# A mixture-of-experts block on one core: big buffers at new addresses, splits of 2048 columns, and another order of work in expert block 0

## What is computed

```python
logits = hf @ w_router + b_router
top_vals, top_idx = lax.top_k(logits, 4); gates = softmax(top_vals)
# tokens sorted by expert into blocks of 128 rows, one expert a block
gu = xb @ w_gate_up[e] + b_gate_up[e]          # 1024 -> 2048
gate = minimum(gu[:, :1024], 7.0); up = clip(gu[:, 1024:], -7.0, 7.0)
act = (up + 1) * (gate * sigmoid(1.702 * gate))
y = act @ w_down[e] + b_down[e]                # 1024 -> 1024
out = segment_sum(y * gate_weight, token)      # and x is added
```

## Time and profile before

| | |
|---|---|
| profiled execution | 1751.46 us, span of the core 1749.6 us |
| runs | 1752.5 to 1759.7, median 1757.2 us |
| granted TensorE clock, mean | 0.987 |
| TensorE busy | 1700.0 us |
| VectorE busy | 1426.3 us |
| ScalarE busy | 1076.2 us |
| GpSimd busy | 248.2 us |
| HBM traffic | 468.66 MB read, 21.67 MB written |

### The profile page before, as it was taken

The page is one execution under the profiler, slowest core; times in us unless marked ns, Lnnn a source line. Parts: engine busy times, 40 slices in busy tenths (PEclk is TensorE's granted clock), DMA queues, the critical chain, the costliest instruction groups (busy, mean ns, idle before and its releaser), DMA issues.

```text
span 1749.6 us, 24667 instructions
## 1 busy us (share of the span) xinstructions
PE 1700.0 (97%) x7969; PEld 1365.6 (78%) x7969; DVE 1426.3 (82%) x1595; ACT 1076.2 (62%) x1325; POOL 248.2 (14%) x179
## 2 busy tenths in 40 slices
PE   7999999999996899999999999999999999999995
PEld 5797777788894678888888888888888888888884
DVE  4864555542528699999999999999999999999994
ACT  5323343422334477877777777777777777777773
POOL 0000000330003731121111211111111111112110
PEclk9999999999997899999999999999999999999998
DMA  8231212333255599999999999999999999999993
GB/s 265 73 97 49 72 50 72 114 97 97 80 200 174 206 372 383 370 372 363 378 372 370 363 370 375 372 368 362 377 371 368 373 361 377 374 368 372 364 375 103
DMA packets 211541, 481.96 MB, mean 275 GB/s; under 512 B 12491, under 2 KB 55027, under 8 KB 194979
## 3 DMA queue, kind: packets, MB, share of 16 engines
q1 hardware_dynamic: 200880, 453.59, 70.4%
q0 software_dynamic: 10624, 27.87, 7.1%
HBM read 468.66 MB, written 21.67 MB: 280 GB/s over the span
## 4 chain that ended last, share of the span: by engine, by line
PE 96%; DVE 2%; DMA 1%; issue 0%; ACT 0%; SPq 0%; POOL 0%; ACTq 0%; DVEq 0%; POOLq 0%
PE ps L573 29%; PE ps L575 28%; PE ps L574 28%; PE ps L774 2%; PE ps L756 2%; PE ps L750 2%; PE ps L686 1%; PE ps L665 1%; PE ps L674 1%; PE ps L648 1%; PE ps L805 0%; PE ps L718 0%; DMA work<-in_k_norm_g 0%; PE ps L593 0%; PE ps L709 0%
## 5 line engine op out<-in xcount | busy, mean ns | idle before, releaser
L1228 DVE TENSOR_TENSOR zT<-raw,zT 128x1024 fp32r<-128x1024 f32 x192 | 228.2, 1230 | 14.6 <-ACT zT L987 11.8
L1228 DVE TENSOR_TENSOR zT<-more_raw,zT 128x1024 fp32r<-128x1024 f32 x192 | 231.7, 1221 | 0.0
L1228 DVE TENSOR_TENSOR w_lo<-more_raw,w_hi 128x1024 fp32r<-128x1024 f32 x192 | 223.3, 1217 | 7.3 <-ACT w_hi L987 7.3
L1228 DVE TENSOR_TENSOR w_lo<-raw,w_hi 128x1024 fp32r<-128x1024 f32 x192 | 223.3, 1216 | 3.3 <-ACT w_hi L987 2.6
L573 PE MATMUL ps<-w_hi,xT 128*128 128x512 f32 x512 | 219.7, 429 | 0.0
L573 PE MATMUL ps<-zT,xT 128*128 128x512 f32 x512 | 205.9, 402 | 0.0
L574 PE MATMUL ps<-w_lo,xT 128*128 128x512 f32 x512 | 204.2, 399 | 0.0
L575 PE MATMUL ps<-w_hi,xT 128*128 128x512 f32 x512 | 203.8, 398 | 0.0
L574 PE MATMUL ps<-zT,xT 128*128 128x512 f32 x512 | 203.0, 397 | 0.0
L575 PE MATMUL ps<-zT,xT 128*128 128x512 f32 x512 | 202.7, 396 | 0.0
L987 ACT ACTIVATE zT<-more_raw 128x1024 fp32r<-128x1024 f32 x192 | 197.6, 1047 | 0.8 <-PE ps L575 0.8
(11 more groups left out here) (240 smaller groups left out, 3385.1 us busy)
## 6 DMA issues: line engine op xcount, KB each, us to landing
more_raw<-in_w_gate_up SPq DMA_DIRECT2D x129, 1024.0 KB, 5.7
raw<-in_w_gate_up SPq DMA_DIRECT2D x127, 1024.0 KB, 7.8
raw<-in_w_down SPq DMA_DIRECT2D x65, 1024.0 KB, 8.9
more_raw<-in_w_down SPq DMA_DIRECT2D x63, 1024.0 KB, 8.2
raw<-in_w_in SPq DMA_DIRECT2D x29, 1024.0 KB, 5.4
r<-in_x SPq DMA_DIRECT2D x8, 512.0 KB, 7.3
raw<-in_w_branch_conv SPq DMA_DIRECT2D x4, 1024.0 KB, 4.9
raw<-in_w_out SPq DMA_DIRECT2D x4, 1024.0 KB, 4.9
```

The lines of the kernel that those rows point to most:

```text
L1228: nc.vector.tensor_tensor(expert_unit(1, pos), chunk[:, UH * (pos % 2):UH * (pos % 2) + UH], expert_unit(0, pos).bitcast(F32), ALU.subtrac ...
```

## The change

Buffers: the small tables are allocated ahead of the big buffers, with a filler of 64 bytes, so that the tables and the filler take 3968 bytes. Before, `raw` started at byte 16512 of a partition and `hT`, `more_raw` at 194496; now `raw` starts at 20480 and every big buffer at a multiple of 4096.

Splits in the expert blocks: one instruction of 2048 columns for a chunk on each engine instead of two of 1024. ScalarE computes 7 - gate with a Relu from PSUM and the sigmoid from that; VectorE multiplies min(gate, 7) by it from PSUM. Chunks 0 and 1 of the next block are split at the end of a block, and `store_y` stands ahead of the splits.

Router and block 0: the one-hot is made for experts 0 and 1, so that block 1's index comes from the same matmuls and its gather is issued before the record scatters (`gather(3)`); the low parts of block 0's rows come before `place_records`; the down biases are four matmuls of 32 rows in four row groups, for one half of the columns each, with a copy of `b_down` for each group, and `add_down_bias` adds four banks at once.

```diff
+        fill = sb("fill", [P, FILL])
         raw = sb("raw", [P, RAW, CH])
...
+            for b in range(NB):
+                sp.dma_start(bdn[NE * b:NE * b + NE, :], b_down[0]).then_inc(down_bias_in, 16)
...
+            def down_bias(n):
+                for b in range(NB):
+                    last = pe.matmul(ps[:, bk_D + b, :], gT[NE * b:NE * b + NE, :],
+                                     bdn[NE * b:NE * b + NE, 512 * n:512 * n + 512], start=True, stop=True)
...
                 if j == 3:
                     pe.wait_ge(gates_ok, 1)
+                    pe.transpose(ps[:, bk_D, 0:P], gmat.rearrange("p b e -> p (b e)"), ident).then_inc(gT_pe, 1)
+                if j == 7:
+                    pe.wait_ge(down_bias_in, 16 * NB)
                     down_bias(0)
+                if j == 11:
+                    pe.wait_ge(x2_biased, 1)
                     down_bias(1)
...
+            def split_expert(g, c):                      # ScalarE
+                sc.wait_ge(used, unit_base(g) + (2 * c - XUN + 2))
+                nc.scalar.activation(expert_pair(0, c), chunk, ACT.Copy).then_inc(split_hi, 2)
...
+                nc.scalar.activation(g1b, ps[:, bk_A + 2 * half, :], ACT.Relu, scale=-1.0,
+                                     bias=stat[:, 24:25]).then_inc(gate_clamped, 1)
...
+                nc.vector.tensor_scalar(uix[:, 0:4:3], ps[:, bk_T, 0:2], float(OUT_OF_RANGE), None,
...
+            split_expert(0, 1)                           # VectorE, after the index
             for half in range(2):
                 ve.wait_ge(turned_hi, half + 1)
...
+            split_expert(0, 2)
+            place_records()
+            gates()
...
+            for c in range(3, 8):
+                split_expert(0, c)
+                if c == 3:
                     gates_by_expert()
...
+            split_expert(1, 0)
+            split_expert(1, 1)
             turned(0, ROWS0, xTh[:, 0:4, :], xTl[:, 0:4, :], bk_T)
...
             gather()                                     # GpSimd
+            gp.wait_ge(turned_pe, FIRST_ROWS)
+            gather(3)
...
-            gather_next(0)
             over_experts()
```

More of the change, by code:

```diff
@@ L445, in expert_unit, with expert_pair @@
             return zT[:, i, 2 * (slot - UN):2 * (slot - UN) + 2, :].rearrange("p k s -> p (k s)")
+        def expert_pair(i, c):
+            slot = 2 * c % XUN
+            if slot < UN:
+                return (w_hi, w_lo)[i][:, slot:slot + 2, :].rearrange("p u h -> p (u h)")
+            return zT[:, i, 2 * (slot - UN):2 * (slot - UN) + 4, :].rearrange("p k s -> p (k s)")
         def packed(t, n):
@@ L735, in _ @@
             last.then_inc(ranks_pe, 1)
[L736 to L739, removed]
+            for e in range(2):
+                pe.wait_ge(hot_ok, e + 1)
+                for b in range(NB):
+                    last = pe.matmul(ps[:, bk_T, e:e + 1], hot[:, e, b, :], cst[:, C_TOK + b:C_TOK + b + 1],
+                                     start=(b == 0), stop=(b == NB - 1))
             last.then_inc(turned_pe, 1)
@@ L997, in _ @@
                                      scale=small[:, 34 + k:35 + k]).then_inc(h2T_a, 1)
-            for j in range(6):
-                split_expert(0, j)
+            for c in range(3):
+                split_expert(0, c)
             sc.wait_ge(logitsT_pe, 1)
@@ L1005, in _ @@
             nc.scalar.activation(gate, gate, ACT.Exp).then_inc(gate_exp_ok, 1)
-            for j in range(6, XUN):
-                split_expert(0, j)
+            for c in range(3, XUN // 2):
+                split_expert(0, c)
             for half in range(2):
@@ L1251, in _ @@
                                                ALU.mult, ALU.mult).then_inc(h2_ok, 1)
-            for j in range(2):
-                split_expert(0, j)
+            split_expert(0, 0)
             ve.wait_ge(logit_rows_pe, 1)
@@ L1346, in _ @@
                                     ALU.add).then_inc(blocks_ok, 1)
-            place_records()
-            gates()
-            for j in range(4, 6):
-                split_expert(0, j)
             for half in range(2):
```

198 lines of the change are left out of this document (95 added, 103 removed).

## The result

The changed kernel takes 1745.7 us in the median of seven runs (1744.2 to 1748.5), the kernel before 1758.0 (1752.5 to 1760.7). The ratio is 0.9935, with a 95% interval from 0.9921 to 0.9949: 0.65% faster. The profiled execution has a span of 1743.2 us (before: 1749.6). The runs of the kernel before fall in two groups, 14 of 40 at 1751.5 to 1754.5 us, with the profiled execution among them, and 26 at 1756.2 to 1760.7.

A forecast was written before the change was run, and what follows sets the result against it. TensorE was taken to bound the steady blocks, matmul following matmul without a gap. From the median of 1757.2 us, -19 for the buffers moved and +5 for blocks 0 and 1 gave 1743 us, range 1700 to 1766.

The forecast's parts named there:

- Buffers moved: Expert blocks and front: aligned xT and hT bring gate_up and hT matmuls to down's start distance, 226.9 ns; -19 us.
- Case D: All matmuls: every start distance falls, because starts at a multiple of 4096 are better than at 128; 1690 us, 12%.
- Wide splits at nothing: Expert blocks: wide splits and ScalarE's gate clamp change no period; zero, bounds -0 and +0.3 us a block.
- Block 0's start: Router to block 0: earlier xT low halves and quicker index start it at 551.6 instead of 554.5, -2.9 us.
- The gates' wait: Within block 0: TensorE has unit 3 done at 560.1 and waits for gates_ok until 562.4; +2.4 us, new.
- Down biases: Within block 0: matmuls in four row groups take 1.2 us twice, -5.8 us; the clock's 2.4 us loss goes too.
- Block 1's start: Behind block 0: block 1 starts at about 585 instead of 598.3, -13 us at that point.
- Landing of block 2's gather: GpSimd's chain during blocks 0 and 1: rows land at 629.7 instead of 610.7, so TensorE waits 17 us.
- Net of block 0 and 1, +5: Blocks 0 and 1: the late gather turns the -13 us into +5 us; bounds -12 and +15.
- B: gate_up at down's distance, but GpSimd hardly held up, block 1 waiting at most 3 us; 1726 us, 13%.
- C: Expert blocks: xT's place changes nothing, the rest as in A; 1762 us (1746 to 1768), 22%.
- A: The forecast: gate_up at down's distance, block 0's gain eaten by block 2's gather; 1743 us (1730 to 1756), 45%.

The follow-up runs named there:

- the first experiment: Kernel before with 64 unused bytes ahead of hT, more_raw and xT, so that these start at a multiple of 128, nothing else moved: 1757.7 us, ratio 1.0002.
- filler before xT: Kernel before with only 64 unused bytes put ahead of hT, more_raw and xT; the same run as the first experiment: 1757.7 us, period 36.01 us.

## Why the prediction was right, and where its steps were not

The median was to fall by 14 us and fell by 12.3; the forecast case (gate_up at down's distance, block 0's gain eaten by block 2's gather) is what the trace shows. That the number came so close was luck in part: between the profiled executions, from which the sum was made, the fall is 6.4 us and not 14.

- **Buffers moved, -19.** In the loop 0.53 us a block, 0.55 predicted. The front gave nothing: its distances fell to 226.7 as predicted, but it ends only 0.3 us earlier (519.3 instead of 519.6). The matmuls with hT that start at 147.8 us in before start at 148.7 here, so up to there the shorter distances bring nothing, and only behind it the front gains, 1.2 us. That term was about 2 us too large; measured, the placing is -15.5 to -17.2. The reason given was wrong in one word: not "a multiple of 128", which the first experiment refutes, but the distance between the two sides, modulo 256. It didn't matter for the time, as the change does both, but that is luck: xT moved to a multiple of 128 alone, by 64 bytes, would have brought nothing.
- **Case D** fell with that: the layout at 4096 gives no distance below 226.7 ns, so none of the places tried brings anything of the way from there to 213.3. D's own sum is 1695 us by its terms, not 1690. No run showed the 215.7 ns of the Trainium skill (TensorE: Matmul & The Clock Gate, section Wait — 56ns, not 53.3ns?).
- **Wide splits at nothing.** Right for the period: no change at distance 0, at most 0.05 us a block at 64. As an instruction that GpSimd meets, a wide split is not free: 5.8 us in the scatters, 5.8 in over_experts. The prediction had this as "Each waits for the other" for over_experts, and didn't ask what twice the length does to the scatters; it took +3, and they came out at +2.7, which fits only because in the kernel before they hadn't been at their least either (26.5 us for 16, one of them 4.70).
- **Block 0's start**, 551.6 predicted, 553.4 measured. The index was to come 0.9 us earlier and came 0.8 later: the saving on VectorE was counted, the second lookup's eight records on TensorE (16 in 3.57 us) weren't, though the index waits for both. With banks and semaphores of their own it is earlier.
- **The gates' wait**, 2.4 predicted, 3.5 measured. **Down biases**, 1.2 us each predicted, 1.14 measured. Their clock cost was put at 2.4 us. In all five kernels with the old block 0 the clock fell to 0.50 around one of the two groups (in before from about 571 us on, in "filler before xT" from about 584), but with one row group in the new order it stayed at 1.00; the narrow matmuls alone don't bring it down, and what else is needed is open.
- **Block 1's start**, 585 predicted, 589.3 measured: the 1.8, 1.1 and some smaller ones add up.
- **Landing of block 2's gather**, 629.7 predicted, 633.2 measured. Records ready +9.0 (7.4 predicted), over_experts +10.6 (8), the two landings +6.5 (3), the gather itself 6.8 us instead of 9.4. The wait was exactly as predicted, 16.9 us against 17, because both its ends were 4 us late.
- **Net of block 0 and 1, +5.** By the medians everything but the placing costs 3.0 us at distance 0 and 5.1 at 64 (1.5 of these in the period), so the term was right or up to 2 us too large, and the -19 was 2 to 3.5 too large the other way; the two errors partly cancel. In the profiled executions block 2 starts 7.7 us later. The prediction summed against an execution of before with the shortest landings seen, and took the difference over to the median unchanged: 5.7 us were added for before, while the changed kernel's median is 0.7 us above its profiled execution. So about 6 of the 12.3 us are no gain between the two traces.

The range, 1700 to 1766, was set by cases B, C, D. The rows at hand couldn't have told C from A: moving xT by 64 bytes gains nothing, moving it by 192 gains 16 us.

## What to carry to other kernels

When only one operand's buffer differs between a fast and a slow matmul, vary its distance to the other operand's buffer, modulo 256 bytes, before blaming its own address. Put GpSimd work with inputs in SBUF where VectorE idles, and keep VectorE's instructions short where a critical chain of small GpSimd instructions and scatters must run beside it: getting over_experts out of the way of the gather and of the splits gave 13.7 us, nearly as much as the placing. And ask of a profiled execution whether its landings are typical before a sum is made against it.

## What the runs showed of the hardware that was not expected

- Matmuls of 512 columns start 226.7 ns apart with the two operands' buffers a multiple of 256 bytes apart, 233.0 with 64 bytes more, 232.3 with 128 (xT standing); with hT streaming 226.7, 228.8 and 233.1. The absolute start doesn't count: a block takes 35.59 us with the big buffers at multiples of 128 and 35.57 with all of them 64 bytes off.
- The waits for the records' landing and for the slot table's ran from 1.5 to 5.4 and from 1.4 to 5.1 us, below 2 us where at most 39 GB/s were moving and above 2.5 where at least 164 were (that the transfers are the cause isn't shown); 1.46 + 1.49 and 4.41 + 4.51 stand in kernels whose code differs by a filler alone.
- The issue of an indirect scatter on GpSimd depends on what VectorE does: 16 of them, 0.97 us each at the least, took 29.1 us beside splits of 2.28 us and 23.3 us beside splits of 1.22 us.
- Eight records of 32-row matmuls take 1.14 us in four row groups, 3.69 in one, at a granted clock of 1.00.
